# The second block's SSD mixer written as a table of steps: projections in halves, and the last tap of the convolution on ScalarE

## The reference

```python
# second block, layer 1 (12 heads of 64, 2 groups, state 128, chunks of 128)
h = rms_norm(x, mix_norm[1])
z, xbc, dt_raw, q_mem = split(h @ b_w_in[0])             # widths 768, 1280, 12, 256
xbc = silu(causal_depthwise_conv(xbc, conv_w, conv_b))   # 4 taps and a bias
xs, bm, cm = split(xbc)                                  # 768, 256, 256
dt = softplus(dt_raw + dt_bias);  da = -dt * exp(a_log)
y  = ssd_scan(xs, dt, a, bm, cm) + xs * d_skip           # decays exp(cs[t] - cs[s]), C.B, masked
y  = rms_norm(y * silu(z), out_norm)
m  = softmax(q_mem @ k_mem.T / 8) @ v_mem                # memory attention, 4 heads of 64
x  = x + concat(y, m) @ w_o[1]

# PEER, after the mixer of each layer: 8 heads, 16 experts a head and token
q = rms_norm(x, ffn_norm) @ w_q
e, gate = top16_of_product_keys(q, sub_keys)
act = gelu(einsum('td,thkd->thk', xn, u[e])) * gate      # xn: the normalised x
x  = x + einsum('thk,thkd->td', act, v[e])               # u, v: 16384 rows of 1024
```

## Time and profile before

| | |
|---|---|
| three executions | 3017.92, 3014.90, 3019.11 us |
| median | 3017.92 us |
| the profiled execution | 3016.67 us, of which the span from the first to the last recorded instruction is 3014.1 us |
| granted TensorE clock, mean | 0.94 |
| TensorE busy | 2473.4 us (82% of the span) |
| VectorE busy | 1425.9 us (47%) |
| ScalarE busy | 889.7 us (30%) |
| GpSimd busy | 699.4 us (23%) |
| read from HBM | 1098.78 MB, 366 GB/s over the span |
| chain that ended last | DMA 44%, PE 40%, DVE 9% |

### The profile page before, as it was taken

How to read it: one execution, slowest core, us unless ns; L and a number is a source line. 1 busy time by engine, 2 the same in 40 slices (tenths; PEclk the granted TensorE clock), 3 DMA queues, 4 the chain that set the end, 5 groups by cost and what they waited for, 6 DMA issues and landing times.

```text
span 3014.1 us, 33539 instructions
## 1 busy us (share of the span) xinstructions
PE 2473.4 (82%) x11846; PEld 1329.6 (44%) x11846; DVE 1425.9 (47%) x3374; ACT 889.7 (30%) x2348; POOL 699.4 (23%) x626
## 2 busy tenths in 40 slices
PE   9999765657999965666798998898987989877777
PEld 8776311113978421212574445454543545422222
DVE  3363100002355201000348876678657786677674
ACT  0231100000122100000235554457334583344333
POOL 4020000001211000000003553324334243444442
PEclk9999978878999988878899999999999999999999
DMA  6337999999434899999839999999999999999997
GB/s 277 126 140 306 427 428 428 428 429 404 179 130 160 367 428 427 428 427 428 359 116 415 419 413 421 422 422 416 417 422 422 417 397 415 421 422 421 420 417 308
DMA packets 123654, 1105.16 MB, mean 367 GB/s; under 512 B 13760, under 2 KB 19296, under 8 KB 23776
## 3 DMA queue, kind: packets, MB, share of 16 engines
q1 hardware_dynamic: 48032, 562.98, 44.9%
q0 software_dynamic: 73728, 536.90, 43.1%
q10 hardware_dynamic: 1728, 3.14, 0.3%
HBM read 1098.78 MB, written 4.19 MB: 366 GB/s over the span
## 4 chain that ended last, share of the span: by engine, by line
DMA 44%; PE 40%; DVE 9%; ACT 3%; issue 3%; POOL 0%; DVEq 0%; SPq 0%; ACTq 0%; POOLq 0%
DMA wbuf<-in_puv,ar 19%; PE ps L759 16%; PE ps L1583 9%; DMA wbuf<-in_w_expert_up 8%; DMA wbuf<-in_w_expert_down 8%; DMA wbuf<-in_w_expert_gate 5%; PE ps L950 4%; PE ps L1130 3%; DVE wbuf L2445 2%; PE ps L915 2%; PE ps L763 2%; ACT ar L2508 2%; ACT L2508 1%; DMA Y<-in_mem 1%; DMA wbuf<-in_w_mem_kv 1%
## 5 line engine op out<-in xcount | busy, mean ns | idle before, releaser
L1583 PE MATMUL ps<-wbuf,ar 128*128 128x512 f32 x1960 | 928.2, 612 | 188.1 <-ACT ar L2508 187.4
L2445 DVE CUSTOM_DVE_ANT_0 wbuf<-wbuf,Y 128x1024 f32<-128x1024 f32 x490 | 602.0, 1229 | 316.9 <-DMA wbuf<-in_puv,ar 308.3
L3152 POOL DMA_INDIRECT wbuf<-in_puv,ar x490 | 541.3, 1105 | 814.6 <-PE ps L1583 710.2
L1130 PE MATMUL ps<-wbuf,ar 128*32 128x512 f32 x2944 | 456.7, 756 | 293.3 <-DMA wbuf<-in_w_expert_up 112.9
L1583 PEld LDWEIGHTS ps<-wbuf,ar 128*128 128x128 f32 x1960 | 355.7, 193 | 692.0 <-issue 690.8
L2508 ACT ACTIVATE ar<-ar 128x1 f32<-128x1 f32 (+1 forms) x1051 | 269.5, 256 | 615.7 <-DVE ar L2445 592.2
L759 PE MATMUL ps<-HT,wbuf 128*128 128x128 f32 (+1 forms) x2640 | 406.3, 311 | 4.3 <-DMA wbuf<-in_w_mem_kv 3.1
L759 PEld LDWEIGHTS ps<-HT,wbuf 128*128 128x128 f32 x2640 | 368.8, 191 | 52.0 <-issue 19.9
L1130 PEld LDWEIGHTS ps<-wbuf,ar 128*32 128x32 f32 x2944 | 92.5, 124 | 642.9 <-issue 204.3
L2505 ACT COPY ar<-ps 128x512 f32<-128x512 f32 (+4 forms) x164 | 75.0, 457 | 710.5 <-PE ps L1130 307.1
L3111 POOL TENSOR_TENSOR sm<-sm,co 128x1 f32<-128x1 f32 x18 | 10.5, 582 | 1116.0 <-DVE sm L1618 1115.8
(11 more groups left out here) (206 smaller groups left out, 2064.4 us busy)
## 6 DMA issues: line engine op xcount, KB each, us to landing
wbuf<-in_w_expert_down SPq DMA_DIRECT2D x64, 2048.0 KB, 31.6
wbuf<-in_w_expert_up SPq DMA_DIRECT2D x62, 2048.0 KB, 31.5
wbuf<-in_w_expert_gate SPq DMA_DIRECT2D x58, 2048.0 KB, 30.6
wbuf<-in_w_in SPq DMA_DIRECT2D x20, 2048.0 KB, 9.0
wbuf<-in_peer_w_q SPq DMA_DIRECT2D x14, 2048.0 KB, 11.7
wbuf<-in_w_o SPq DMA_DIRECT2D x6, 2048.0 KB, 11.6
wbuf<-in_b_w_in SPq DMA_DIRECT2D x6, 2048.0 KB, 11.4
wbuf<-in_w_branch_b SPq DMA_DIRECT2D x4, 2048.0 KB, 7.9
```

Source lines behind the costliest of these rows:

```text
L1130: m = T.e.matmul(ps(jobs[n])[32 * k:32 * k + 32, :], lhs(c, k), v[:, 512 * n:512 * n + 512], start=(c == 0), stop=(c == 7), tile_position= ...
L1583: m = T.e.matmul(acc[n][:, :], DG[:, j % 4, :], rows_of(name)[:, 1024 + 512 * n:1536 + 512 * n], start=(j == 0), stop=(j == 127))
L2445: V.did(V.e.tensor_tensor_reduce(u, u, Y[:, i, :], 1.0, 0.0, ALU.mult, ALU.add, DT[:, i, j:j + 1]), f"dot{l}{i}.{j}")
L3152: G.land(G.e.indirect_dma_start(out=rows_of(name), out_offset=None, in_=I["puv"], in_offset=bass.IndirectOffsetOnAxis(ap=IX[:, i, j:j + 1] ...
```

## The change

`mix_b(i)` becomes, on each of the three engines, one loop over the step number with an `if` for every part, and the parts are laid out anew:
- Projections: `x0` and `x4` are made in halves, two chunks a step, in steps 5 to 8; `cs` and `x8` follow in 8 and 9; `z4` in two halves of 256 columns in 10 and 11, `z5` in 12.
- Memory attention: scores in 9 and 10, maxima 10 and 11, exponentials 11 and 12, root 12 and 13, transposes 14 and 15, `unit_out` 15 and 16, values 17 and 18.
- Convolution: ScalarE's `raw` also writes, for each channel group, tap 3 times the value plus the bias, as an `Identity` activation straight from PSUM; VectorE adds the three other taps. `raw` is in steps 7, 9, 10, the convolution in 8 to 12, its Silu in 14 as before.
- The SSD part starts a step later (`xs` and `cb` in 16, `e` in 17 to 22, `ym` in 21 to 26), with three buffers for the decays in place of two and one more step between a decay and its use.
- Norm and output: VectorE has `tr` in 27, mean 28, reciprocal root 29, `turn_tile` 30, adds `r0` in 32; ScalarE has the square in 28, the root 29, the scaling 30; TensorE turns in 31 and makes `r0` in 32 and `r1` in 34. The mixer has 35 steps in place of 32, so `prep_tile` starts three steps later.
- `cs.out` comes from VectorE's step 11 and `cs` itself in TensorE's step 8.

```diff
-        bEE = cbuf[:, 0, 0:1024].rearrange("p (k h n) -> p k h n", k=2, h=2)
+        bEE = [v.rearrange("p (h n) -> p h n", h=2)
+               for v in (cbuf[:, 0, 0:512], cbuf[:, 0, 512:1024], cbuf[:, 1, 1024:1536])]
...
TensorE
+            def chunks_of(job, i, v, c0, ks, last, *names):
+                b = take(job) if ks[0] == 0 else ps(job)
+                for k in ks:
+                    m = mm(b[:, 128 * k:128 * k + 128],
+                           [(v[:, c, c0 + 128 * k:c0 + 128 * k + 128], HT[:, c, 128 * i:128 * i + 128]) for c in range(8)])
+                if last:
+                    T.did(m, job, *names)
...
-                for j in range(2):
-                    chunks_tile(f"{p}x{4 * j}", i, tile(f"{p}w{1 + j}"), 0, 4, f"{p}w{1 + j}.used")
-                    yield
...
+                for n in range(35):
...
+                    if n in (5, 7):
+                        chunks_of(f"{p}x{2 * n - 10}", i, tile(f"{p}w{n // 2 - 1}"), 0, (0, 1), False)
+                    if n in (6, 8):
+                        chunks_of(f"{p}x{2 * n - 12}", i, wtile(f"{p}w{n // 2 - 2}"), 0, (2, 3), True, f"{p}w{n // 2 - 2}.used")
+                    if n == 8:
+                        T.wait_ge(*at[p + "da"])
+                        b = take(p + "cs")
...
+                    if n == 9:
+                        T.wait_ge(*at[p + "qm.out"])
+                        chunks_tile(f"{p}x8", i, tile(f"{p}w3"), 0, 2, f"{p}w3.used")
+                    if n in (9, 10):
+                        unit_scores(f"b{i}m", memory[n - 9], n - 9)
+                    if n == 10:
+                        v = tile(p + "w4")
+                        b = take(p + "z4")
+                        mm(b[:, 0:256], [(Hi[c], v[:, c, 0:256]) for c in range(8)])
+                    if n == 11:
+                        T.did(mm(b[:, 256:512], [(Hi[c], v[:, c, 256:512]) for c in range(8)]), p + "z4", p + "w4.used")
+                    if n == 12:
+                        v = tile(p + "w5")
+                        b = take(p + "z5")
...
+                    if n in (14, 15):
+                        unit_turned(f"b{i}m", memory[n - 14], n - 14)
+                    if n == 16:
+                        T.wait_ge(*at[p + "xc"])
...
+                    if n in (17, 18):
+                        unit_values(f"b{i}m", memory[n - 17], n - 17)
+                    if 17 <= n < 23:
+                        hp = n - 17
                         b = take(f"{p}e{hp}")
...
+                    if n == 20:
+                        for k in range(2):
+                            take(f"{p}y{k}", keep=True)
+                    if 21 <= n < 27:
+                        hp = n - 21
+                        T.wait_ge(*at[f"{p}ee{hp}"])
...
+                    if n == 31:
+                        T.wait_ge(*at[p + "y"])
+                        turn_tile(f"b{i}o", Y[:, i, 0:768], 6)
+                    if n in (32, 34):
+                        half = n // 2 - 16
...
VectorE
-                    ts(bXC[:, c, :], bXR[:, c, 0:128], w[0], gain("convb", c), ALU.mult, ALU.add)
-                    for k in range(1, 4):
-                        stt(bXC[:, c, :], bXR[:, c, k:k + 128], w[k], bXC[:, c, :], ALU.mult, ALU.add,
+                    for k in range(3):
+                        stt(bXC[:, c, :], bXR[:, c, k:k + 128], pf[:, k0 + 10 * k + c:k0 + 10 * k + c + 1], bXC[:, c, :],
...
+                    if 8 <= n < 13:
+                        convolve(i, (2 * n - 16, 2 * n - 15))
+                    if n in (10, 11):
+                        unit_max(f"b{i}m", memory[n - 10], n - 10)
+                    if n == 11:
+                        V.wait_ge(*at[p + "cs"])
+                        ts(b_nac, ps(p + "cs")[:, 0:12], -1.0, None, ALU.mult, None, *([p + "cs.out"] if i else []))
...
+                    if n in (12, 13):
+                        unit_root(f"b{i}m", memory[n - 12], n - 12)
...
+                    if 19 <= n < 25:
+                        hp = n - 19
+                        V.wait_ge(*at[f"{p}ex{hp}"])
+                        e = bEE[hp % 3][:, :, lo:256]
...
+                    if n == 27:
+                        V.wait_ge(*at[f"{p}ym5"])
...
+                    if n == 28:
+                        mean_row(f"b{i}o", 768)
+                    if n == 29:
+                        rstd_row(f"b{i}o")
+                    if n == 30:
+                        turn_tile(f"b{i}o", i, "outn", 6)
+                    if n == 32:
+                        residual_half(i, 0)
+                    yield
+                residual_half(i, 1)
...
ScalarE
-                    copy(bXR[:, c:c + n, 3:131], ps(f"{p}x{c}")[:, 0:128 * n].rearrange("p (k t) -> p k t", k=n), f"{p}x{c}.out")
+                    x = ps(f"{p}x{c}")
+                    copy(bXR[:, c:c + m, 3:131], x[:, 0:128 * m].rearrange("p (k t) -> p k t", k=m))
+                    for k in range(m):
+                        w = pf[:, k0 + 30 + c + k:k0 + 31 + c + k]
+                        act(bXC[:, c + k, :], x[:, 128 * k:128 * k + 128], ACT.Identity, *([f"{p}x{c}.out"] if k + 1 == m else []),
+                            scale=w, bias=gain("convb", c + k))
...
+                    if n == 7:
+                        raw(0, 4)
+                    if n == 9:
+                        raw(4, 4)
+                    if n == 10:
+                        raw(8, 2)
+                    if n in (11, 12):
+                        unit_exp(f"b{i}m", memory[n - 11], n - 11)
+                    if n == 12:
+                        gate(4, 0, 512)
+                    if n == 13:
+                        gate(5, 512, 256)
...
+                    if 18 <= n < 24:
+                        hp = n - 18
+                        A.wait_ge(*at[f"{p}tm{hp}"])
+                        if hp > 2:
+                            A.wait_ge(*at[f"{p}ym{hp - 3}"])
...
+                    if n == 28:
+                        A.wait_ge(*at[p + "tr"])
+                        square_row(f"b{i}o", bTR, Y[:, i, 0:768])
+                    if n == 29:
+                        root_row(f"b{i}o")
+                    if n == 30:
+                        A.wait_ge(*at[f"b{i}o.r"])
+                        act(Y[:, i, 0:768], bTR, ACT.Copy, p + "y", scale=small(425, 1))
                     yield
```

More of the change, by code:

```diff
@@ L1448, in mix_b @@
                 Hi = [HT[:, c, 128 * i:128 * i + 128] for c in range(8)]
-                for _ in range(3):
-                    yield
-                T.wait_ge(*at[f"b{i}n.y"])
-                turn_tile(f"b{i}n", Y[:, i, :], 8)
-                yield
-                for c in (0, 4):
-                    T.wait_ge(*at[f"b{i}n.t{c}.out"])
-                v = tile(p + "w0")
-                chunks_tile(p + "qm", i, v, 12, 2)
-                b = take(p + "dt")
-                T.did(mm(b[:, 0:12], [(Hi[c], v[:, c, 0:12]) for c in range(8)]), p + "dt", p + "w0.used")
@@ L1472, in mix_b @@
-                next(memory_steps)
-                yield
-                next(memory_steps)
-                chunks_tile(f"{p}x8", i, tile(f"{p}w3"), 0, 2, f"{p}w3.used")
-                yield
-                for j, n in ((4, 512), (None, 0), (5, 256)):
-                    next(memory_steps)
-                    if j:
-                        v = tile(f"{p}w{j}")
-                        b = take(f"{p}z{j}")
-                        T.did(mm(b[:, 0:n], [(Hi[c], v[:, c, 0:n]) for c in range(8)]), f"{p}z{j}", f"{p}w{j}.used")
-                    yield
@@ L1484, in mix_b @@
-                drain(memory_steps)
-                for _ in range(3):
-                    yield
-                T.wait_ge(*at[p + "xc"])
-                for c, m_ in ((0, 4), (4, 2)):
-                    b = take(f"{p}xs{c}")
-                    for k in range(m_):
-                        m = tr(b[:, 128 * k:128 * k + 128], bXC[:, c + k, :])
-                    T.did(m, f"{p}xs{c}")
-                b = take(p + "cb")
-                if i == 1:
-                    T.wait_ge(*at["b0.b0"])
@@ L1522, in mix_b @@
-                for n in range(2):
-                    release(f"{p}y{n}")
-                for _ in range(3):
-                    yield
-                T.wait_ge(*at[p + "y"])
-                turn_tile(f"b{i}o", Y[:, i, 0:768], 6)
-                yield
-                for c in (0, 4):
-                    T.wait_ge(*at[f"b{i}o.t{c}.out"])
-                Oi = Hi[0:6] + [aOM[:, i, 128 * c:128 * c + 128] for c in range(2)]
-                for half in range(2):
-                    v = tile(f"{p}wo{half}")
-                    b = take(f"{p}r{half}")
-                    T.did(mm(b[:, :], [(Oi[c], v[:, c, :]) for c in range(8)]), f"{p}r{half}", f"{p}wo{half}.used")
-                    yield
-                    if half == 0:
-                        yield
+                memory = with_bufs(mem_units(f"b{i}m", 1, bQM, 1), tb_b, pb_b[i])
@@ L2355, in mix_b @@
[L2355 to L2370 removed]
+                    if n == 27:
```

(20 more changed lines are left out.)

316 lines of the change are left out of this document (137 added, 179 removed).

## The result

| | executions | median | range |
|---|---|---|---|
| before | 5 | 3017.31 us | 3014.9 to 3019.11 |
| after | 5 | 3048.42 us | 3046.06 to 3053.71 |
| ratio | | 1.0102 | 95% interval 1.009 to 1.0113 |

The change costs 31.1 us by the medians. The direction was forecast, a loss, but of 15.1 us; the measured time lies 0.4 us above the range's end of 3048. The profiled execution's span is 3047.0 us, 32.9 more than before.

The account below looks back on a forecast made before the run. The prediction took the last 1440 us as bound by transfers (gathers and weights). Halves -1.3, last tap 0, bank wait 5.0 and tail 11.4 made +15.1 us on 3016.67, a median of 3033, range 3012 to 3048.

Parts of the forecast that it names:

- What bounds the kernel: The last 1440 us are bound by transfers; a better mixer can win at most about 8.8 us (0.29%).
- Projections in halves: Steps 3 to 12: TensorE's work stays the same, more even steps gain 1.3 us.
- Last tap and bias on ScalarE: Convolution: VectorE loses 3.8 us a tile, ScalarE gains 3.7, no table load for Identity; taken as 0.
- The PSUM ring: TensorE's step 10: `z4` waits some 10 us for the bank of `cs`; 5.0 us for both tiles.
- Steps 18 to 27: Decays, sorting, gate and residual, second tile: six steps take 37.2 us, steps 24 to 27 take 22.4.
- Steps 28 to 32: Output norm and product: producer and consumer share a step or are reversed; 33.2 us from gather 56 to `wo0` free.
- Signs: Expected in each tile: `z4` idle 8 to 12 us, VectorE idle 5 to 6, rate under 400 GB/s for some 60.
- The 11.4 us: From gather 36 to `wo0` free: 7.1 + 4.3 us without new requests in the two tiles; bounds 0 and 16.
- the waits of `prep_tile`: Steps 35 to 38: its norm is skewed too, but `wq0` and `wq1` feed the DMA engines; priced at 0.
- its weakest step: How much of the waits the ten row buffers absorb.
- The sum: All priced moves together: +15.1 us against the profiled execution's 3016.67 us, a median of 3033.
- rival C: Bank wait with clock fall, 12 us a tile, fully exposed beside the 11.4 us: 3053 us; chance 0.10.

Follow-up runs that it names:

- c_whole: `a_both` with the projections whole again (x0 in step 5, x4 in 7, z4 in 10): 3018.86 us, ratio 1.0002.
- c_taps: `a_both` with the last tap and the bias back on VectorE: 3016.73 us, ratio 0.9998.
- a_tail: The changed kernel with output norm, output product and `prep_tile` one step earlier on ScalarE and TensorE: 3025.52 us, ratio 1.0021.
- a_both: The repaired kernel: the changed kernel with the edits of `a_cs` and `a_tail` together: 3020.7 us, ratio 1.0007.
- a_cs: The changed kernel with VectorE reading `cs` out in its step 9 in place of 11: 3039.2 us, ratio 1.0070.
- c_prep_late: `a_both` with `prep_tile` alone one step late again on ScalarE and TensorE: 3019.01 us, ratio 1.0000.
- c_pair: `a_both` with the decay exponentials of two pairs in one visit to the exponential table: 3018.75 us, ratio 1.0001.
- d_dve_tail: `a_cs` with VectorE's whole tail, `prep_tile` included, one step later, all 35 steps kept: 3019.51 us, ratio 1.0001.

## Why the prediction was right or wrong

- **What bounds the kernel**: right. The last 1440 us are bound by transfers, and the loss lies in the windows where the rate fell. No version came under the kernel before by more than its interval, as the 0.29% of room suggested.
- **Projections in halves**, taken as a gain of 1.3 us: nothing that can be measured (`c_whole`).
- **Last tap and bias on ScalarE**, taken as 0: right (`c_taps`). The price of one was low: 459 ns, not 367, so 4.6 us a tile. The row taken was of an exponential with a bias for each partition; the Identity has a scale for each partition as well, which may be the difference (no run separates the two). No table was loaded for Identity; in the second tile's step 7, ScalarE's copy and four Identity activations stand with no load before or behind:

```profile
2368.18 0.59 ACT L2509 COPY ar<-ps 128x512 f32<-128x512 f32 x1
2368.80 1.94 ACT L2512 ACTIVATE ar<-ps,pf 128x128 f32<-128x128 f32 x4
```

  The Trainium skill (ScalarE: Activation LUTs, Table sets: the hidden batching unit) has identity as a filler in every set; these rows agree.
- **The PSUM ring**: mechanism, place and length of the wait right, price too low. TensorE was there 69.5 us after the stage's first dot product (2392.2 against 2322.7; forecast 70), the wait was 9.55 and 10.59 us (forecast 10), ended by VectorE on `cs`. It was priced at 5.0 us for both tiles with bounds of 0 and 12; taken out of the changed kernel it gives 9.7 us, by the stages 12.8, at or over the upper bound. Without the skew, in `a_tail` against `a_both`, it costs 4.2 us (1.0021 - 1.0007; 4.4 by the stages), though TensorE still waits 9.65 and 12.28 us for it: the 5.0 is near the price of this wait when it stands alone.
- **Steps 18 to 27**, second tile: the period right, the sum 4.4 us too long. The table loads of the decays are 6.2 us apart (2456.01 to 2462.24), from the dot product of gather 36 (2445.61) to that of gather 56 (2500.79) are 55.2 us; forecast 59.6.
- **Steps 28 to 32**: mechanism right, too short. From gather 56 to `wo0` free were forecast 33.2 us, it was 39.8 (`wq0` requested at 2540.55). Missing is the clock: the two groups of eight table records took 6.73 and 6.41 us in place of 3.67, 5.8 of the 6.6 us. The first of them delays the transposes, and so VectorE's idle before its copy was 8.49 us and not 5 to 6. The whole stretch from gather 36 was 94.9 us for 92.8; `wq0` came 117.2 us after `wo1` (2423.35), in the first tile 113.1, just under the forecast of 115 to 125:

```profile
2423.35 0.33 SPq L541 DMA_DIRECT2D wbuf<-in_w_o  x1
...
2540.55 0.33 SPq L541 DMA_DIRECT2D wbuf<-in_peer_w_q  x1
```

- **Signs**: a rate under 400 GB/s was forecast for some 60 us of each tile; the windows above have 90 us of it in each.
- **What failed** is the step behind the request of `wq0`. The 11.4 us were taken as all of the tail, and the waits of `prep_tile` at nothing, "then `wq0` and `wq1` are there to feed the DMA engines, so I price it at 0". The count itself came out: in `a_cs`, without the bank's wait, `wo0` is free 89.5 and 91.9 us after gather 36, and less the 69.0 and 70.8 of before and twice 14.9 that leaves 11.8 us. But the whole tail cost 20.8 us (18.3 by the stages; 24.4 while the bank's wait was in), above the upper bound of 16. Put level, `prep_tile` alone gives back 13.0 us (10.7): its waits come on top of the norm's, when little of the gathers in flight is left. In the repaired kernel, with short waits ahead of it, the zero was right. A second thing was left out: VectorE adds `r0` in the step of its product, where before it stood a step behind, and waits 11.68 us for it in place of 3.25. With `r1` it is the same move, yet there the wait hardly changed, 6.21 for 6.16.
- **The prices were taken one by one**, as if the bank's wait, the norm's and `prep_tile`'s did not draw on the same gathers in flight. The prediction called this its weakest step.
- **The sum**: -1.3 + 0 + 5.0 + 11.4 = 15.1 was forecast; measured are about 0, 0, 9.7 and 20.8, 30.5 of the 31.1 us (12.8 and 18.3 by the stages). The time that came is near rival C's 3053, and for half of C's reason: C had the bank's wait at 12 us a tile, 24 in all, and 11.4 for the tail.

## What to carry to other kernels

When parts of a program are moved on several engine queues, write the shift of each engine beside the others before looking at any duration: here +2 against +3 was the greater part of the loss, and moving the output norm's rows and all behind them one step earlier on ScalarE and TensorE, or one step later on VectorE, brought it back. Look at every pair of producer and consumer that comes to share a step: here VectorE waited 11.68 us for a product of 6.9 us in its own step, and still 3.25 us with the product a step ahead. Do the same for a ring of buffers: `z4` took the bank that VectorE read out three steps behind its writing, and waited 10 us. And do not price waits ahead of a buffered stream one by one. In this kernel about 15 us of VectorE's idle a tile cost nothing that can be measured, and what came on top of 19 us in the second tile cost at least its length (the first tile was less clear). Sum the waits of one stretch first, and compare the sum with what the transfers in flight last.

## What had not been expected of the hardware

The start of the first PEER stage lies at 1574.76 us in the profiled execution before and at 1586.78 in that of `a_tail`, the ends of what the fourteen profiled executions show, though no edit touches what runs ahead of it. That is 12 us, more than the whole effect of some of these edits; its cause stays open. VectorE's timeline, before and `a_tail`:

```profile
1574.76 1.23 DVE L2445 CUSTOM_DVE_ANT_0 wbuf<-wbuf,Y 128x1024 f32<-128x1024 f32 x1 [1.85 <-DMA wbuf<-in_puv,ar]
```

```profile
1586.78 1.22 DVE L2449 CUSTOM_DVE_ANT_0 wbuf<-wbuf,Y 128x1024 f32<-128x1024 f32 x1 [1.80 <-DMA wbuf<-in_puv,ar]
```

The length of a changed stage repeats to about 1 us between kernels that cost the same there (369.8 to 370.9 for (1,0), 375.2 to 375.4 for (0,1), in `a_both`, `c_prep_late`, `c_taps`, `c_whole`, `c_pair` and `d_dve_tail`), and told more than the medians did. Each is one profiled execution, so these lengths have no interval of their own.
